# One-hot matrices of a dense expert stage, built in batches of 8 tokens instead of blocks of 4

## The reference, cut to what matters

```
e = i1[...] * N_KEYS + i2[...]                  # expert number: row e1 = e // 128, column e2 = e % 128
g = softmax(sc)                                 # 128 weights for each token
act = einsum('td,tkd->tk', xt, u_tab[et])
out = einsum('tk,tkd->td', gelu(act) * gt, v_tab[et])
```

## Time and profile before

| | |
|---|---|
| time, median of 3 runs | 1743.4 us (1741.38 to 1743.91) |
| span of the profiled execution, first to last instruction | 1738.7 us |
| busy: PE, DVE, ACT, POOL | 1666.5, 1554.8, 866.7, 654.3 us |
| G stage, by DVE's first and last one-hot | 536.9 to 657.8 us |

### The profile page before, as it was taken

How to read it: one execution, slowest core, us unless ns; L and a number is a source line. 1 busy time by engine, 2 the same in 40 slices (tenths; PEclk the granted TensorE clock), 3 DMA queues, 4 the chain that set the end, 5 groups by cost and what they waited for, 6 DMA issues and landing times.

```text
span 1738.7 us, 29907 instructions
## 1 busy us (share of the span) xinstructions
PE 1666.5 (96%) x9344; PEld 1402.2 (81%) x9344; DVE 1554.8 (89%) x3196; ACT 866.7 (50%) x2431; POOL 654.3 (38%) x644
## 2 busy tenths in 40 slices
PE   6999999999966999999999999999999999999997
PEld 4566777866645788899989999999999988999996
DVE  3887863499999999999999999999999999999998
ACT  3222564346778995444444444444444444444443
POOL 0000000034557994444444444344444444443442
PEclk9999999999977999999999999999999999999999
DMA  9343202211135779999999999999999999999996
GB/s 357 125 141 123 74 1 78 71 61 49 61 121 173 223 201 346 396 389 401 408 395 401 405 407 401 403 409 395 396 407 399 396 406 400 402 402 403 400 400 211
DMA packets 129316, 505.91 MB, mean 291 GB/s; under 512 B 9184, under 2 KB 64096, under 8 KB 79968
## 3 DMA queue, kind: packets, MB, share of 16 engines
q0 software_dynamic: 36864, 268.45, 38.3%
q1 hardware_dynamic: 92096, 236.49, 36.5%
q10 hardware_dynamic: 288, 0.13, 0.0%
HBM read 477.18 MB, written 25.10 MB: 289 GB/s over the span
## 4 chain that ended last, share of the span: by engine, by line
DVE 35%; DMA 23%; PE 19%; issue 19%; ACT 2%; POOL 2%; DVEq 1%; SPq 0%; POOLq 0%; ACTq 0%
DMA slab<-table,ixr 22%; DVE slab L1745 9%; PE psum L501 7%; DVE slab L1695 5%; DVE ulo L1636 4%; PE psum L736 3%; DVE slab L1735 3%; DVE slab L1699 2%; DVE vlo L1722 2%; DVE slab L1730 2%; PE psum L502 2%; PE psum L666 1%; DVE wlo L1718 1%; POOL slab L1876 1%; DVE slab L1550 1%
## 5 line engine op out<-in xcount | busy, mean ns | idle before, releaser
L1876 POOL DMA_INDIRECT slab<-table,ixr x256 | 421.5, 1647 | 603.8 <-DVE slab L1745 552.2
L848 PE MATMUL psum<-hhi,uhi 128*128 128x384 f32 x1008 | 338.8, 336 | 2.4 <-issue 2.1
L848 PE MATMUL psum<-hhi,ulo 128*128 128x384 f32 x1008 | 338.2, 335 | 0.0
L848 PE MATMUL psum<-hlo,uhi 128*128 128x384 f32 x1008 | 337.6, 335 | 0.0
L1745 DVE SCALAR_TENSOR_TENSOR slab<-slab,cf 128x1024 f32<-128x1024 f32 x252 | 323.3, 1283 | 14.8 <-DVE slab L1745 0.5
L1735 DVE SCALAR_TENSOR_TENSOR slab<-slab,h2tok 128x1024 f32<-128x1024 f32 x256 | 312.2, 1220 | 26.5 <-DMA slab<-table,ixr 26.2
L862 PE MATMUL psum<-vhi,whi 128*128 128x512 f32 x762 | 297.1, 390 | 3.1 <-DVE wlo L1718 3.1
L862 PE MATMUL psum<-vhi,wlo 128*128 128x512 f32 x762 | 299.7, 393 | 0.0
L862 PE MATMUL psum<-vlo,whi 128*128 128x512 f32 x762 | 299.2, 393 | 0.0
L501 PE MATMUL psum<-slab 128*128 128x512 f32 x464 | 239.1, 597 | 2.1 <-ACT slab L929 1.7
L1210 ACT CAST whi<-slab 128x384 fp32r<-128x384 f32 x127 | 65.3, 514 | 306.7 <-DVE slab L1730 306.7
(11 more groups left out here) (237 smaller groups left out, 2801.3 us busy)
## 6 DMA issues: line engine op xcount, KB each, us to landing
slab<-ublk SPq DMA_DIRECT2D x64, 1024.0 KB
slab<-vtab SPq DMA_DIRECT2D x63, 1024.0 KB
slab<-wblk SPq DMA_DIRECT2D x90, 512.0 KB, 4.6
g_dram<-slab SPq DMA_DIRECT2D x11, 1984.0 KB, 9.0
slab<-g_dram SPq DMA_DIRECT2D x31, 704.0 KB, 8.9
slab<-table,ixr POOLq DMA_INDIRECT x256, 9.2
slab<-slab SPq DMA_DIRECT2D x42, 64.0 KB, 10.1
x<-x_in SPq DMA_DIRECT2D x1, 2560.0 KB, 9.6
```

The costliest lines, as they stand in the source:

```text
L848: last = pe.matmul(psum[:, b, 0:ND], w[:, c, :], m[:, c, :], start=(m_ == 0), stop=(m_ == 3 * DC - 1))
L1876: pool.indirect_dma_start(out=rows[:, sl % GR, :], out_offset=None, in_=table, in_offset=bass.IndirectOffsetOnAxis(ap=ixr[:, half, half_co ...
```

## The change

G is built in 48 batches of 8 tokens, with two buffers of each kind.
- DVE makes, for each batch, `same` (1 where e2 equals k, for all 8 tokens, 128 x 1024, bf16, from a new bf16 table iota8 and a new bf16 copy e2b of the columns), and all 8 rows of hot_a in one tensor_tensor (128 x 1024, float32). In batches 2 and 3 it also makes 4 of the rows of hot_b.
- POOL no longer makes rows of hot_a. It multiplies `same` with gT for 7 of the 8 tokens in one tensor_tensor (128 x 896, bf16 and float32 in, float32 out, written with the key as the outer and the token as the inner loop, 512 bytes apart). In batches 2 and 3 it makes 3 rows and issues two of the indirect DMAs.
- ACT makes one row of hot_b in 8 (before: 1 in 4) and copies the banks as before.
- PE's matmuls and their banks are the same; it reads the rows from the batch's buffer and waits for POOL at the first half of a batch, for ACT's row at the second.
- iota8 is filled once ahead of the selection; e2b costs DVE one cast more for each of the 3 tiles.

```diff
-FETCH_AT = (2, 3, 4, 5)
+BATCH = 8
+NB = ND // BATCH
+FETCH_IN = (2, 3)
+OWN = BATCH - 1
...
+            def by_vector(n):
+
+                return BATCH // 2 if n in FETCH_IN else 0
...
             for b in range(ND // 4):
-                pe.wait_ge(hot_a_set, sum(hot_a_split(n) > 0 for n in range(b + 1)))
-                pe.wait_ge(hot_b_set, b + 1)
-                pe.wait_ge(hot_c_set, b + 1)
+                at, half = divmod(b, 2)
+                if half:
+                    pe.wait_ge(hot_c_set, at + 1)
+                else:
+                    pe.wait_ge(hot_a_set, at + 1)
+                    pe.wait_ge(hot_b_set, at + 1)
+                    if at in FETCH_IN:
+                        pe.wait_ge(hot_d_set, FETCH_IN.index(at) + 1)
...
+            step(v.tensor_copy(iota8[:], con[:, C_IOTA:C_IOTA + KEYS].unsqueeze(2).broadcast_to([P, KEYS, BATCH])))
...
+                step(v.tensor_copy(e2b[:, part], e2u[:]))
...
+            def hot_batch(n):
+                col, b = first_token(n), n % 2
+                if n >= 2:
+                    v.wait_ge(hot_b_set, n - 1)
+                if n - 2 in FETCH_IN:
+                    v.wait_ge(hot_d_set, FETCH_IN.index(n - 2) + 1)
+                v.tensor_tensor(same[b], iota8[:], e2b[:, col:col + BATCH].unsqueeze(1).broadcast_to([P, KEYS, BATCH]), ALU.is_equal).then_inc(same_set, 1)
+                if n >= 2:
+                    v.wait_ge(g_made, 2 * n - 2)
+                wide = [P, BATCH, KEYS]
+                v.tensor_tensor(hot_a[:, b], con[:, C_IOTA:C_IOTA + KEYS].unsqueeze(1).broadcast_to(wide),
+                                e1T[:, col:col + BATCH].unsqueeze(2).broadcast_to(wide), ALU.is_equal).then_inc(hot_a_set, 1)
+                m = by_vector(n)
+                if m:
+                    v.wait_ge(same_set, n + 1)
+                    v.tensor_tensor(hot_b[:, b, 0:m].rearrange("p t k -> p k t"), same[b][:, :, 0:m],
+                                    gT[:, col:col + m].unsqueeze(1).broadcast_to([P, KEYS, m]), ALU.mult).then_inc(hot_d_set, 1)
...
-                    for m in range(hot_a_split(b)):
-                        last = pool.tensor_scalar(hot_a[:, b % 4, m, :], con[:, C_IOTA:C_IOTA + KEYS], e1T[:, col + m:col + m + 1], None, ALU.is_equal)
-                    last.then_inc(hot_a_set, 1)
+            for n in range(NB):
+                col, b, m = first_token(n), n % 2, by_vector(n)
+                if n % (P // BATCH) == 0:
+                    pool.wait_ge(slot_set, n * BATCH // P + 1)
+                if n >= 2:
+                    pool.wait_ge(g_made, 2 * n - 2)
+                pool.wait_ge(same_set, n + 1)
+                pool.tensor_tensor(hot_b[:, b, m:OWN].rearrange("p t k -> p k t"), same[b][:, :, m:OWN],
+                                   gT[:, col + m:col + OWN].unsqueeze(1).broadcast_to([P, KEYS, OWN - m]), ALU.mult).then_inc(hot_b_set, 1)
```

More of the change, by code:

```diff
@@ L207, in build @@
         eT = sb("eT", [P, ND], U32)
+        iota8 = sb("iota8", [P, KEYS, BATCH], BF16)
+        e2b = sb("e2b", [P, ND], BF16)
         e1T, e2T, gT = (sb(n, [P, ND]) for n in ("e1T", "e2T", "gT"))
@@ L263, in build @@
         e1u, e2u = (view(n, P).bitcast(U32) for n in (0, P))
-        gnT, away = view(38016, ND), view(256, 4, KEYS)
+        gnT, away = view(38016, ND), view(2816, 2, KEYS)
+        same = [view(c0, KEYS * BATCH // 2).bitcast(BF16).rearrange("p (k t) -> p k t", t=BATCH) for c0 in (256, 37248)]
         v_raw0 = view(35584, D)
-        hot_a, hot_b = view(9216, 4, 4, P), view(3072, 4, 4, P)
+        hot_a, hot_b = view(9216, 2, BATCH, P), view(3072, 2, BATCH, P)
         gbuf = view(19456, 2, KEYS, TG)
@@ L826, in _ @@
                 for m in range(4):
-                    last = pe.matmul(psum[:, 4 + b % 4, m * P:(m + 1) * P], hot_a[:, b % 4, m, :], hot_b[:, b % 4, m, :], start=True, stop=True)
+                    last = pe.matmul(psum[:, 4 + b % 4, m * P:(m + 1) * P], hot_a[:, at % 2, 4 * half + m, :], hot_b[:, at % 2, 4 * half + m, :], start=True, stop=True)
                 last.then_inc(g_made, 1)
@@ L1145, in _, with distance, hot_row @@
                 act.activation(gnT[:, t * P:(t + 1) * P], psum[:, SLOT_BANK[k], P:2 * P], ACT.Copy, scale=-1.0).then_inc(slot_set, 1)
[L1147 to L1160, removed]
+            def distance(n):
+                if n % (P // BATCH) == 0:
+                    act.wait_ge(halves_set, n * BATCH // P + 1)
+                col = first_token(n) + OWN
+                if n >= 2:
+                    act.wait_ge(hot_c_set, n - 1)
+                act.activation(away[:, n % 2, :], con[:, C_IOTA:C_IOTA + KEYS], ACT.Abs, bias=e2T[:, col:col + 1], scale=-1.0).then_inc(away_set, 1)
+            def hot_row(n):
+                col = first_token(n) + OWN
+                act.wait_ge(away_set, n + 1)
+                if n >= 2:
+                    act.wait_ge(g_made, 2 * n - 2)
+                act.activation(hot_b[:, n % 2, OWN, :], away[:, n % 2, :], ACT.Relu, bias=gT[:, col:col + 1], scale=gnT[:, col:col + 1])\
                     .then_inc(hot_c_set, 1)
@@ L1175, in _ @@
             act.wait_ge(slot_set, N_DENSE)
[L1176 to L1179, removed]
+            for n in range(2):
+                distance(n)
+            hot_row(0)
             for b in range(ND // 4):
[L1181 to L1184, removed]
+                at, half = divmod(b, 2)
+                if not half and at + 2 < NB:
+                    distance(at + 2)
+                if half and at + 1 < NB:
+                    hot_row(at + 1)
                 group, m = divmod(b, TG // 4)
@@ L1688, in _ @@
             for k in range(N_DENSE):
                 v.wait_ge(slot_set, k + 1)
[L1690 to L1701, removed]
+                for n in range(k * P // BATCH, (k + 1) * P // BATCH):
+                    hot_batch(n)
+                    within = n % (P // BATCH)
@@ L1702, in _ @@
                     if k + 1 < N_DENSE:
-                        if within == 18:
+                        if within == 9:
                             split_number(k + 1)
-                        elif within == 20:
+                        elif within == 10:
                             number_halves(k + 1)
-                        elif within == 22:
+                        elif within == 11:
                             halves_ready()
-                    if k == 0 and within == 0:
+                    if n == 0:
@@ L1710, in _ @@
                         late_sums()
-                    elif k == 0 and within == 1:
                         row_numbers()
@@ L1895, in _ @@
             pool.wait_ge(h2_tok, 2 * N_GATHER)
[L1896 to L1908, removed]
-                    for m in range(hot_a_split(b)):
-                        last = pool.tensor_scalar(hot_a[:, b % 4, m, :], con[:, C_IOTA:C_IOTA + KEYS], e1T[:, col + m:col + m + 1], None, ALU.is_equal)
-                    last.then_inc(hot_a_set, 1)
+            for n in range(NB):
+                col, b, m = first_token(n), n % 2, by_vector(n)
+                if n % (P // BATCH) == 0:
+                    pool.wait_ge(slot_set, n * BATCH // P + 1)
+                if n >= 2:
+                    pool.wait_ge(g_made, 2 * n - 2)
+                pool.wait_ge(same_set, n + 1)
+                pool.tensor_tensor(hot_b[:, b, m:OWN].rearrange("p t k -> p k t"), same[b][:, :, m:OWN],
+                                   gT[:, col + m:col + OWN].unsqueeze(1).broadcast_to([P, KEYS, OWN - m]), ALU.mult).then_inc(hot_b_set, 1)
+                if n == FETCH_IN[0]:
+                    pool.wait_ge(row_numbers_set, 1)
+                    pool.tensor_copy(ixr[:, 0, :], idxf[:, 0:8]).then_inc(ix_copied, 1)
+                    pool.wait_ge(ix_copied, 1)
+                if n in FETCH_IN:
+                    for sl in (2 * FETCH_IN.index(n), 2 * FETCH_IN.index(n) + 1):
+                        fetch_row(sl, 0, sl)
             pool.wait_ge(uhi_set, 4)
```

11 lines of the change are left out of this document (4 added, 7 removed).

## The result

The changed kernel takes 1793.26 us (median of 4 runs, 1791.18 to 1795.71), the kernel before 1742.39 on the same chip (4 runs, 1739.78 to 1743.91): 1.0295 times as long, with an interval of 1.028 to 1.031. It is 50.9 us slower by the medians. The profiled execution has a span of 1790.7 us at a granted clock of 0.984, where before had 1738.7 at 0.986: 52.0 us.

A forecast was written before the change was run, and what follows sets the result against it. DVE was taken to bound the G stage, whose length moves the kernel's end one for one. 48 x 3.48 = 167.0, small work 3.5, e2b 0.6 and end 1.2 make 172.3 against 121.1: + 51 us, 1794, range 1778 to 1824.

The forecast's parts named there:

- Two-input operations of POOL and DVE shut each other out: G stage: DVE's same and hot_a and POOL's product, each reading two SBUF operands, cannot run together, so their times add.
- the three places in the prediction: Trace before the change, at 514.91, 662.33 and after: DVE and POOL operations lengthened, read as one shutting the other out.
- The period is the sum of the three: G stage, each batch of 8 tokens: same 0.61, hot_a 1.13 and POOL's product 1.74 add to 3.48 us, against 2.45.
- I take 1.74, because the types are those of L1852: POOL's product of 896 elements: 1.74 us, from bf16 with float32 products at 1.74 ns an element plus 0.17.
- The bound of 2.8 us from L1857: POOL's strided product: 638 ns for 200 elements, 3.2 ns each, would make 2.8 us for 896; kept for the range.
- DVE and POOL together fill the stage: Sign that the forecast is right: DVE and POOL together, not each, fill the G stage.
- 3.5 a batch, the same: Batches 2 and 3: DVE's product and compares, 2.35 us, lie under POOL's two issues, 2.6; POOL's product 0.84.
- no lasting fall of clock: PE in the G stage: would be busy 2.4 of 3.48 us, so its clock was expected not to fall lastingly.
- No shutting out: Rival for the G stage: DVE and POOL run side by side, PE sets the period; 13 us faster, 1730; 5 in 100.
- partial overlap: Rival: POOL holds its path for only half the product; period 2.8, 19 us slower, 1762; 8 in 100.
- POOL slow at this layout: Rival: strided product takes 2.8 us, period 4.5, time 1844; leaves the range from 2.5 us on; 13 in 100.
- The change does nothing: Rival: PE or ACT set the G stage's pace, period 2.4 and not 3.5; 2 in 100.

The follow-up runs named there:

- rows_in_psum: The changed kernel with the expert rows e1, one of hot_a's two operands, kept in a PSUM bank instead of SBUF: 1754.81 us, ratio 1.0077 to the kernel before.
- both_in_psum: As rows_in_psum, with e2 moved to PSUM too, as float32: 1744.72 us, ratio 1.0015 to the kernel before.
- pool_writes_only: The changed kernel with POOL's product replaced by a memset of the same elements, so G is wrong there: 1734.4 us, ratio 0.9961 to the kernel before.
- one_weight: both_in_psum with one value of gT as second operand of POOL's product for all 896 elements: 1742.26 us, ratio 1.0003 to the kernel before.
- product_dense: The changed kernel with POOL's product written in one dense run, not 512 bytes apart: 1791.69 us, ratio 1.0278 to the kernel before.
- copy_more: The changed kernel with one more DVE copy of 512 columns from PSUM to PSUM in each batch: 1793.28 us, ratio 1.029 to the kernel before.

## Why the prediction was right

The direction, the mechanism and the size came out: 1793.26 against 1794.0, where the page showed 52.0 us more for the 51 of the sum. Part of the nearness is the median's distance from the span, which I had put at 4.7 and which is 2.6 this time (1793.26 - 1790.7). By its steps:

- **What bounds the kernel, and what hangs on the stage.** Right. The stage's end moved by 51.85 us and the kernel's by 52.0.
- **Two-input operations of POOL and DVE shut each other out.** Right, and shown: a small operand moved to PSUM takes 0.85 us off POOL's product (rows_in_psum), a second one frees `same` (both_in_psum), and so does a POOL that only writes (pool_writes_only). "With two-input operations" was too narrow, though: the last of the three places in the prediction, L1742 at 2882 ns, is a tensor_scalar with one tensor operand, and the runs show the same for DVE's casts and tensor_scalars from SBUF to SBUF, beside the product and beside the fill. The prediction had rested the inclusion of the bf16 compare on a page alone; the trace now agrees with the Trainium skill (SBUF — State Buffer, section "Who interferes with whom"): 2.43 us beside the product, 0.69 at the start of the stage, before POOL had anything to do.
- **The period is the sum of the three.** Right at 3.49 us for 3.48, but two terms were off in opposite directions, by more than the total. The step that was mis-sized is "I take 1.74, because the types are those of L1852": the product works for 1.88 in the changed kernel and takes 1.95 undisturbed. It was not the types. The types are the same in one_weight, where the second operand is a single value, and there 0.15 of the 0.21 is gone; in L1852 it stays the same over an inner run, in this product it changes with each element. With its fixed cost the undisturbed product is 1950 / 896 = 2.2 ns an element, between L1852's 1568 / 800 = 2.0 and the float32 row's 2352 / 1024 = 2.3 in the earlier trace rows. Against it, `same` costs 0.47 in the chain and not 0.61, and a product 1.88 and not 1.95. I put that down to each having already started when the path comes free, so that its start-up lies under the wait; the numbers are read, this reason is argued.
- **The bound of 2.8 us from L1857.** It was not the stride: product_dense leaves the product at 2790 ns. That bound held the range open for nothing.
- **Nothing hides behind DVE's busy share.** "DVE and POOL together fill the stage" was right, and copy_more shows how it is to be read: 0.69 us of DVE's standing time in each batch is free for work that has no operand in SBUF.
- **Batches 2 and 3, "3.5 a batch, the same".** Wrong by 3.4 us. Products 2, 3 and 4 start at 545.90, 552.45 and 556.27: 10.37 us for two batches, not 7.0. DVE in order of time, from the changed kernel:

```profile
553.48 0.69 DVE L1707 TENSOR_TENSOR slab<-iota,e2b 128x1024 bf16<-128x1024 bf16 x1 [0.74 <-POOL slab L1924]
...
555.61 1.22 DVE L1711 TENSOR_TENSOR slab<-con,e1T 128x1024 f32<-128x1024 f32 x1 [1.44 <-PE psum L836]
...
558.67 2.41 DVE L1707 TENSOR_TENSOR slab<-iota,e2b 128x1024 bf16<-128x1024 bf16 x1 [1.84 <-POOL slab L1924]
...
561.93 1.23 DVE L1711 TENSOR_TENSOR slab<-con,e1T 128x1024 f32<-128x1024 f32 x1 [0.84 <-PE psum L836]
```

  POOL's issues came to 1.78, 0.94, 1.45 and 0.94 us with 0.99 before the first, and its products queued behind them; DVE then waits for 4.86 us in all. DVE's own product of 512, for which I had 0.61, took 1.66 and 1.04 us, the first of them beside POOL's product. From the end of the cast to e2T (537.74) to the end of the last product (709.20) the stage takes 171.5 us, where the sum had 170.5. Less 48 periods of 3.49 that is 4.0, and less these 3.4 it leaves 0.6 for DVE's small work, which I had put at 3.5. That 0.6 is a balance: where DVE splits the numbers of the next tile the products start 3.75 and 3.89 us apart, in both tiles, 1.3 us in all, and from product 4 to product 7 (556.27 to 565.65) the stage makes up 1.1. Two wrong terms again, with nearly the same total.
- **Start and end.** The stage begins 0.99 us later than before, where e2b was to cost 0.6. This number says little: in the runs whose code ahead of the stage is that of the changed kernel or nearly so, the cast to e2T starts anywhere from 534.76 (copy_more) to 538.35 us (product_dense), and the fill of iota8 is in all of them. The end costs 0.5 us more than before, not 1.2: 3.34 from the last product's end to the row at 712.54, against 2.88 from 657.81 to 660.69.
- **PE, "no lasting fall of clock".** Right from 590 us on: 1.00 in every stretch of 10 us to 710. Before it there are stretches at 0.71 (540 to 550), 0.86 (560 to 570) and 0.83 (580 to 590); PE had stood 2.79 us before its matmuls at 553.55 and 3.17 before those at 558.74. The products still start 3.49 us apart at 0.83 (580.26, 583.75, 587.24).
- **The rivals.** No shutting out and partial overlap both fall: `same` ends only after POOL has done its 1.88. POOL slow at this layout falls by rows_in_psum and product_dense. The change does nothing falls by the period. Two of their prices were worked out wrongly, which changes no verdict: with half of the product beside DVE the period is 3.48 - 0.87 = 2.61 and not 2.8, some 10 us more than before and not 19; and a slow product leaves the range from 1.74 + (1824 - 1794) / 48 = 2.4 us on, not 2.5.

Where the Trainium skill was weighed (GPSIMD Engine Reference, section 3.1: an estimate of 1.94 us for the product), the undisturbed product agrees with it: 1.95. Put into my sum it would still have given a worse time, 10 us too late, because `same` and the product each lose 0.07 to 0.14 at the handover. The two errors of my sum cancelled; a hit within 1 us is partly luck.

## What to carry to other kernels

Before widening work on DVE and handing its twin to POOL, look at what each reads from SBUF. A DVE compare with two operands there and a POOL product add their times here, so price such a period as a sum and not as the larger of the two. DVE's casts and tensor_scalars from SBUF to SBUF were held as well, and these even by a POOL fill that reads nothing. In the other direction a POOL copy of 8 columns, with one operand, took 0.88 us beside DVE's product of 512 and 0.19 in both_in_psum. The cure was not less work but another place for the smaller operand: from PSUM, the same wide compares run beside POOL, and 50.9 us slower becomes 2.3 slower; with `same` cut to the 7 rows in use it becomes 0.2% faster. And a busy share near 100% on two engines that fit this pattern is no sign of a full engine; look for durations that grow by exactly what the other engine was running.

## What the runs showed of the hardware that was not expected

- A float32 compare on DVE costs the same with one operand in PSUM as with both in SBUF: 1.21 us for 1024 columns both ways.
- POOL's fill of 896 strided float32 takes 1.72 us, hardly less than its product of 1.95. It leaves DVE's two-input compares alone (683 ns for `same`) but holds its casts and tensor_scalars from SBUF to SBUF (0.59 to 0.86 us where they take 0.2 alone), of which this stage has few.
- DVE needs 1.69 us for the product of 896 (1.9 ns an element, 1.7 with start-up overlapped), against 1.2 ns an element for the float32 compares. Its output stride and its bf16 by float32 operands came together here; which of them costs was not tried.
- The stride of POOL's output (512 bytes) costs nothing that shows: 2790 ns dense, 2773 strided, in which 0.92 are waiting.
- With the indirect fetches late, one store of G took 19.5 us to land (median 9.1); with them early the longest took 14.2.
